# Gate and up weights of the experts in pieces of 4096 bytes, expert rows turned from every fourth column

## What is computed

```python
def _grouped_moe(x, router_w, router_bias, w_gate, w_up, w_down):
    t = x.reshape(-1, d)                      # 512 x 1024
    ...
    hid = jax.nn.silu(jnp.einsum('td,edf->tef', t, w_gate)) * jnp.einsum('td,edf->tef', t, w_up)
    y = jnp.einsum('tef,efd->td', hid * gates.astype(hid.dtype)[..., None], w_down)
```

## Time and profile before

| | us |
|---|---|
| median of 3 runs | 1387.47 (1386.65 to 1389.38) |
| the profiled execution | 1391.02 |
| its span from the first to the last instruction | 1389.2 |
| TensorE products busy in it | 1321.1 (95%) |
| weight loads busy, beside the products | 760.2 (55%) |
| VectorE / ScalarE / GpSimd busy | 790.4 / 351.1 / 303.3 |

### The profile page before, as it was taken

One profiled execution on the slowest core, in us unless ns is written; L12 is line 12 of the kernel. 1 busy time (PEld: TensorE's weight loads), 2 busy tenths in 40 slices (PEclk: granted clock), 3 DMA queues, 4 the chain that ended last, 5 costly groups with the idle time before them and its releaser, 6 DMA issues. The chain is left out here.

```text
span 1389.2 us, 22501 instructions
## 1 busy us (share of the span) xinstructions
PE 1321.1 (95%) x8070; PEld 760.2 (55%) x8070; DVE 790.4 (57%) x1733; ACT 351.1 (25%) x785; POOL 303.3 (22%) x536
## 2 busy tenths in 40 slices
PE   8979999999999999999988999999999999899995
PEld 5449575765757667486746333355545454533332
DVE  2856667676766767775656442284354455644227
ACT  3322322232232222222212221113332322222210
POOL 2254416043250523406012000131000000200025
PEclk9989999999999999999988999999999999999998
DMA  6440414316052250524533999860211119399973
GB/s 211 129 109 14 114 53 137 86 38 188 8 159 65 72 154 8 154 68 129 191 121 114 350 409 412 328 204 1 74 42 43 42 59 362 120 363 413 413 290 114
DMA packets 173480, 220.97 MB, mean 159 GB/s; under 512 B 57377, under 2 KB 107937, under 8 KB 173409
## 3 DMA queue, kind: packets, MB, share of 16 engines
q1 hardware_dynamic: 134464, 166.05, 34.5%
q10 hardware_dynamic: 33856, 35.92, 7.6%
q0 software_dynamic: 5088, 18.02, 3.6%
HBM read 185.63 MB, written 34.34 MB: 158 GB/s over the span
## 5 line engine op out<-in xcount | busy, mean ns | idle before, releaser
L528 PE MATMUL bank<-xT,wgu 128*128 128x512 f32 x448 | 196.5, 596 | 3.1 <-DVE wgu L1226 3.1
L2083 PE MATMUL bank<-wgu,moe_xgT 128*32 128x512 f32 x1536 | 169.8, 594 | 0.8 <-issue 0.4
L528 PEld LDWEIGHTS bank<-xT,wgu 128*128 128x128 f32 x448 | 84.6, 192 | 104.9 <-issue 104.9
L1226 DVE SCALAR_TENSOR_TENSOR wgu<-bank,taps,wgu 128x510 f32<-128x510 f32 (+1 forms) x128 | 95.6, 747 | 65.5 <-ACT wgu L825 59.7
L576 PE MATMUL bank<-wd,oT 128*128 128x512 f32 x256 | 123.1, 607 | 3.8 <-DMA wd<-dn_w_out 2.6
L610 PE MATMUL bank<-wd,xT 128*128 128x256 f32 x512 | 122.0, 389 | 2.8 <-DMA wd<-dn_w_in 2.7
L610 PEld LDWEIGHTS bank<-wd,xT 128*128 128x128 f32 x512 | 96.5, 194 | 19.1 <-issue 3.3
L2083 PEld LDWEIGHTS bank<-wgu,moe_xgT 128*32 128x32 f32 x1536 | 49.1, 110 | 103.2 <-issue 91.1
L2118 PE MATMUL bank<-wd,moe_hidT 128*32 128x512 f32 x768 | 87.0, 593 | 3.4 <-issue 2.2
L2364 DVE TENSOR_TENSOR moe_hid<-moe_silu,bank 128x256 f32<-128x256 f32 x24 | 10.1, 421 | 127.6 <-ACT moe_silu L2207 127.6
L1679 POOL DMA_INDIRECT wgu<-slots_y,fetch x8 | 11.3, 1416 | 274.7 <-DMA slots_y<-moe_y_rows 260.6
(11 more groups left out here) (356 smaller groups left out, 2273.4 us busy)
## 6 DMA issues: line engine op xcount, KB each, us to landing
wgu<-moe_w_gate SPq DMA_DIRECT2D x32, 1024.0 KB, 13.0
wgu<-moe_w_up SPq DMA_DIRECT2D x32, 1024.0 KB, 14.7
wd<-moe_w_down SPq DMA_DIRECT2D x32, 1024.0 KB, 15.5
wgu<-dn_w_in SPq DMA_DIRECT2D x32, 512.0 KB, 3.9
slots_x<-gains SPq DMA_DIRECT2D x5, 1920.0 KB, 10.1
wd<-dn_w_out ACTq DMA_DIRECT2D x16, 512.0 KB, 4.0
xT<-slots_x ACTq DMA_DIRECT2D x16, 512.0 KB, 7.9
wgu<-gate_rows SPq DMA_DIRECT2D x14, 512.0 KB, 5.1
```

Source lines behind the costliest of these rows:

```text
L528: mm = pe.matmul(bank[:], wqkv[:, ct, k], xT[:, k], start=k == 0, stop=k == KD - 1)
L1226: ins = nc.vector.scalar_tensor_tensor(out=conv[:, ct, lo:hi], in0=bank[:, lo + d:hi + d], scalar=w[:, j:j + 1], in1=conv[:, ct, lo:hi], o ...
L2083: mm = pe.matmul(ps[2][seats].rearrange("p (a f) -> p a f", a=2), xgT[:, j % ROW_BUFS, k, seats], wgu[:, e % RING, :, k], start=k == 0, st ...
```

## The change

The gate and up matrices are laid out so that partition `p` holds rows `4p` to `4p + 3` of each block of 512: pieces of 4096 bytes, half as many. `columns` names every fourth column in place of every second, and `gain_cols` comes in pieces of four numbers. `EACH` is a new constant. All that used these helpers follows: `load_gate_up`, lines 1995, 1996, 2022 and 2023 for the transfers, and lines 2069, 2133 and 2162 for the turning.

```diff
-                sp.dma_start(t["gain_cols"][:, layer, j % 2].rearrange("p (c a) -> p c a", a=2), dram[name][layer].rearrange("(c p a) -> p c a", p=P, a=2)).then_inc(t["gain_cols_in"], 16)
+                sp.dma_start(t["gain_cols"][:, layer, j % 2].rearrange("p (c a) -> p c a", a=EACH), dram[name][layer].rearrange("(c p a) -> p c a", p=P, a=EACH)).then_inc(t["gain_cols_in"], 16)
...
+EACH = 4
...
-    gate, up = (dram[name][layer].rearrange("e (k p a) f -> p e k (a f)", p=P, a=2) for name in ("moe_w_gate", "moe_w_up"))
+    gate, up = (dram[name][layer].rearrange("e (k p a) f -> p e k (a f)", p=P, a=EACH) for name in ("moe_w_gate", "moe_w_up"))
...
 def pair_rows(w):
 
-    return w.rearrange("p (k a) f -> p k (a f)", a=2)
+    return w.rearrange("p (k a) f -> p k (a f)", a=EACH)
...
 def columns(rows, k):
 
-    return rows[:, k // 2 * 2 * P:(k // 2 + 1) * 2 * P].rearrange("p (n a) -> p a n", a=2)[:, k % 2]
+    return rows[:, k // EACH * EACH * P:(k // EACH + 1) * EACH * P].rearrange("p (n a) -> p a n", a=EACH)[:, k % EACH]
```

## The result

| | before | after |
|---|---|---|
| median of 4 runs each, us | 1387.06 (1383.62 to 1389.38) | 1399.32 (1397.77 to 1400.99) |
| span of the profiled execution, us | 1389.2 | 1396.0 |
| TensorE products busy, us | 1321.1 | 1332.7 |
| picking of layer 0 / of layer 1, us | 10.50 / 7.74 | 15.13 / 15.13 |
| the 12 passes behind the picking, layer 0 / 1, us | 144.62 / 146.45 | 143.43 / 143.43 |

The ratio is 1.0091 (95% interval 1.0066 to 1.0115): slower, by 12.3 us between the medians, where 30.0 were forecast. The rows of stages are worked out from the starts of records: the picking from its first product to the first product of `gate_up` behind it, the passes from there to the start of the last product of `down`. The columns sum to the spans. (All lines behind the new constant are one higher: 2069, 2083, 2118 and 2133 are now 2070, 2084, 2119 and 2134.)

What follows compares the result with a forecast made beforehand. TensorE was taken to bound the kernel: turning +21.1, picking +7.8 and +4.8, together +33.7 us, less waits of 2.6 and 1.1, net +30.0 on 1387.5, giving 1417.5 us; range 1384 to 1423.

Steps and rivals of the forecast that it cites:

- What bounds the kernel: In both expert stages TensorE's own work sets the time; transfers cost it only some 2.6 us and 1.1 us of waits.
- The transfers: Gate and up loads in 4096-byte pieces: 0.2 us less an expert, worth -2 to -2.6 us through TensorE's waits.
- the waits for weights and for the rows of pass 1: TensorE's stops in the expert stages, expected to vanish: -2.6 us for weights, -1.1 us for rows.
- Rival 4: Gate and up pieces are cut again on the way and stay at 2048 bytes; chance 0.31 together with case of free steps.
- The picking: Line 2133, 64 loads a layer at 240 ns distance: +7.8 us in layer 1, +4.8 us in layer 0.
- The turning: Line 2069's 176 transposes: load distance doubles from 120 to 240 ns, +21.1 us.
- The rule of 16 bytes: For TensorE's strided loads: 8-byte steps free, 16-byte steps penalised; cited as speaking against the change, without a size.
- The middle rival: Each load of turning and picking costs GpSimd's 68 ns more: +14 us, 1401.5 us; chance 0.17 including what lies between.
- The clock on top: First product group behind the picking might run at 1.2 GHz: up to some 3 us a layer, in range, not forecast.

Runs made afterwards that it cites:

- e2: Kernel before, with only the first four experts of each layer at four rows a piece and every fourth column: 1400.5 us, ratio 1.0077.
- e3: The changed kernel itself, measured again beside the others on one chip: 1397.37 us, ratio 1.0054.
- e1: Changed kernel, with the first four experts of each layer kept at two rows a piece and every second column: 1384.04 us, ratio 0.9956.
- e4: Changed kernel with EACH = 8, so eight rows a piece (8192 bytes) and every eighth column: ratio 1.0056.
- e7: Changed kernel with picking and turning by every third column, not matching the weights' rows: picking's load 263 ns, no whole time given.
- e11: Kernel with single rows (1024 bytes) for the first four experts of each layer, eight rows a piece for the others: 1382.77 us, ratio 0.9960 to before.

## Why the prediction was right in its sign and wrong in its size

- **What bounds the kernel: right.** TensorE is the path in both stages; +12.0 us of loads there gave +7.8 us by the stages, with the passes 4.2 us shorter, and e2 and e3 measured +10.7 and +7.5.
- **The transfers: right.** 418 to 420 GB/s for the larger pieces, about 0.2 us less an expert, and the waits for weights and for the rows of pass 1 gone: the passes are 4.2 us shorter where 3.7 were worked out. Rival 4 falls: the packets went from 173480 to 156072, so the pieces weren't cut again. In e1, where nothing gets longer, the passes alone give 2.2 us for a forecast of 2.0 to 2.6.
- **The picking: right in its number, by luck in its reason.** +7.4 and +4.6 us for 7.8 and 4.8, a distance of 233 ns for 240. But the 240 was the doubled distance of the transposes' loads, and a product's load had shown no doubling (192 and 197 ns). That it then grows by 132 ns comes from something that no row of before showed.
- **The turning: this step failed.** "Turning, 176 x (240 - 120) ns = 21.1 us" was some 0.1 to 0.2 us: the load went from 209 to 211 ns, the distance from 120 to 121. The step behind it was "the doubling from one to two doubled the reading, and the one from two to four does so again", worked out on transposes and then applied to both kinds of load. It holds for neither as it was put. A transpose's load has a contiguous level (141 ns) and one for any step (190 to 211 ns at two, three, four and eight). A product's load is as long at one as at two (192 and 197) and grows from two to four. The growth that was seen belonged to the one kind, the growth that came to the other.
- **Was it to be read off before?** Partly: the earlier trace rows had the two kinds side by side, 141 to 209 beside 192 to 197 for the same change of step. They plainly didn't follow one law, and the prediction named the second pair as speaking against its choice but gave both kinds the same bound. Bounded apart, the sum has four corners, and one of them comes near the result: picking doubled, turning free, 30.0 - 21.1 = +8.9 us.
- **The rule of 16 bytes.** The Trainium skill, "Advanced Engine Details and Errata", section SBUF Cachelines, gives two hits on a line as free and one as penalised. For the loads of products this was right where the row of before was silent: 197 ns at two hits, 329 at one, 263 in between. For transposes it is wrong on both sides: two hits cost 68 ns over contiguous, and one hit no more than two (209 and 211).
- **The middle rival** (1401.5 us, from GpSimd's row) came near the measured 1399.3 for no reason of its own: it spread 68 ns over all 304 loads, where the distance of the picking's 128 grew by 115 ns at the upper clock (20 at the lower) and that of the others by 1.
- **The clock on top: not seen.** In layer 0 the granted clock was at its upper level from 754.3 us, in the middle of the picking, and the products behind it took 8.04 us to the next step in both kernels.

What stays open: how large the loss is on average, since 12.3 us were measured once and 7.5 once. The stages of the changed kernel are equal to 0.01 us in both profiles; those of the kernel before were traced only once, and its picking is what moves with the clock. And how the array's two modes read the memory; only their times were measured. The count of 16-byte pieces fits the products' loads from a step of two on; that lines of the memory are the reason is argued from this count and not shown.

## What to carry to other kernels

Count the form of every instruction that a layout reaches, and bound each by rows of its own form: a float32 transpose and a float32 product may load the same columns and not the same way. A layout that makes transfers longer pieces is paid for where somebody reads across it, so look for the one reader outside the main loop; here it was a step of one pass, which the experts loaded ahead could serve with a layout of their own. And a queue that is full in every slice was worth only what the bound engine had waited for it, 2 to 4 us of some 290 in the passes.

## What the runs showed of the hardware

| columns apart | 16-byte pieces touched | product's load, ns | transpose's load, ns |
|---|---|---|---|
| 1 | 32 | 192 | 141 |
| 2 | 64 | 197 | 209 |
| 3 | 96 | 263 | 197 |
| 4 | 128 | 329 | 211 |
| 8 | 128 | 337 | 190 |

All are medians of load records of 128 x 128 float32, of the kernels before, after, e4, e7 and e11. The contiguous transpose's 141 is line 586 of the earlier trace rows; e11's contiguous turnings, from the same tile as the strided ones, have 140. At the lower clock a product's load takes 331 ns at a step of two and 329 at four (213 and 233 apart). That a transpose's load is shorter at a step of three or eight than at two or four was not expected, and nothing here explains it. Pieces of 2048 bytes moved at 405 GB/s, of 4096 at 418 to 421. Inside the stage, the stretch that ran at 412 GB/s with half of its bytes in pieces of 2048, and at 420 with pieces of 4096, ran at 424 in e4, with gate and up in pieces of 8192 and down in 4096:

```profile
820.00:840.00 20.00, 20.00 (x184) 7.52 (x180) 11.03 (x21) 5.04 (x12) 0.00 (x0) 1.00 1.02 424
```
